# A two-block diffusion transformer step on one core: squares of the inner tiles moved to GpSimd, modulation sums spread in eighths

## The reference, cut to what matters

```python
cond = silu(c)
for i in range(2):
    mod = (cond @ ada_w[i] + ada_b[i])[:, None, :]
    sh1, sc1, g1, sh2, sc2, g2 = split(mod, 6)
    h = rmsnorm(x, norm_mix_g[i]) * (1.0 + sc1) + sh1
    y = rglru_mixer(h, ...) if i == 0 else dsa_mixer(h, ...)
    x = x + g1 * y
    h = rmsnorm(x, norm_ffn_g[i]) * (1.0 + sc2) + sh2
    x = x + g2 * (square(relu(h @ ffn_w1[i])) @ ffn_w2[i])
...
# second network, per layer
mod   = silu(c_2) @ w_mod_2[i] + b_mod_2[i]
mod_c = silu(c_ctx_2) @ w_mod_2[i] + b_mod_2[i]
# in rglru_mixer: the decay
log_a = -8.0 * r * softplus(-lam)
```

## Time and profile before

| | |
|---|---|
| median of 3 runs | 4178.69 us (4171.87 to 4182.22) |
| profiled execution, its time | 4176.06 us |
| its span | 4174.3 us |
| mean granted TensorE clock | 0.927 |
| PE busy | 3728.4 us (89%) |
| DVE busy | 1787.4 us (43%) |
| ACT busy | 1277.4 us (31%) |
| POOL busy | 1016.4 us (24%) |
| DMA, mean | 80 GB/s |

### The profile page before, as it was taken

How to read it: one execution, slowest core, us unless ns; L and a number is a source line. 1 busy time by engine, 2 the same in 40 slices (tenths; PEclk the granted TensorE clock), 3 DMA queues, 4 the chain that set the end, 5 groups by cost and what they waited for, 6 DMA issues and landing times. The chain is left out here.

```text
span 4174.3 us, 42210 instructions
## 1 busy us (share of the span) xinstructions
PE 3728.4 (89%) x17052; PEld 2731.1 (65%) x17052; DVE 1787.4 (43%) x3099; ACT 1277.4 (31%) x2258; POOL 1016.4 (24%) x920
## 2 busy tenths in 40 slices
PE   7998999878898898898869988799998999998997
PEld 3446878436477784455668885688887447756885
DVE  7637785275478854502334441412223104422223
ACT  1413222246222224524422222321113334533222
POOL 0223433120133330011034520322222111004443
PEclk8998999989999998989968879899999999999998
DMA  6425543110244431110011101111111111012221
GB/s 264 151 81 191 202 165 127 46 41 1 80 173 165 175 134 53 39 41 21 1 40 40 32 14 71 41 63 66 70 60 46 46 41 56 1 41 74 88 101 61
DMA packets 67043, 333.94 MB, mean 80 GB/s; under 512 B 32352, under 2 KB 35360, under 8 KB 42016
## 3 DMA queue, kind: packets, MB, share of 16 engines
q1 hardware_dynamic: 66416, 328.86, 21.4%
q10 hardware_dynamic: 432, 2.38, 0.1%
HBM read 324.30 MB, written 6.91 MB: 79 GB/s over the span
## 5 line engine op out<-in xcount | busy, mean ns | idle before, releaser
L629 PE MATMUL PSB<-R,R 128*128 128x512 f32 (+1 forms) x2432 | 929.4, 382 | 94.9 <-DVE R L887 48.9
L603 POOL TENSOR_TENSOR R<-SB,R 128x1024 fp32r<-128x1024 f32 x260 | 640.0, 2463 | 1420.5 <-ACT R L594 1420.4
L630 PE MATMUL PSB<-R,R 128*128 128x512 f32 (+1 forms) x2432 | 897.4, 377 | 0.0
L559 PE MATMUL PSB<-SB 128*128 128x512 f32 (+1 forms) x2176 | 843.3, 549 | 23.4 <-ACT SB L1285 18.5
L633 PE MATMUL PSB<-R,R 128*128 128x512 f32 (+1 forms) x2432 | 845.7, 377 | 0.0
L559 PEld LDWEIGHTS PSB<-SB 128*128 128x128 f32 x2176 | 420.7, 194 | 439.2 <-issue 409.7
L629 PEld LDWEIGHTS PSB<-R,R 128*128 128x128 f32 x2432 | 467.2, 192 | 219.3 <-DVE R L1011 31.9
L630 PEld LDWEIGHTS PSB<-R,R 128*128 128x128 f32 x2432 | 467.4, 192 | 79.6
L633 PEld LDWEIGHTS PSB<-R,R 128*128 128x128 f32 x2432 | 437.1, 193 | 65.3
L421 DVE SCALAR_TENSOR_TENSOR SB<-SB 128x512 f32<-128x512 f32 x504 | 473.6, 984 | 7.2 <-DMA SB<-in_ada 2.0
L594 ACT ACTIVATE R<-SB 128x1024 fp32r<-128x1024 f32 x260 | 273.2, 1052 | 551.3 <-PE PSB L633 532.7
(11 more groups left out here) (318 smaller groups left out, 4218.7 us busy)
## 6 DMA issues: line engine op xcount, KB each, us to landing
SB<-in_w SPq DMA_DIRECT2D x95, 2048.0 KB, 8.6
SB<-in_ada SPq DMA_DIRECT2D x96, 1024.0 KB, 5.1
SB<-gate_rows SPq DMA_DIRECT2D x12, 512.0 KB, 4.3
SB<-in_rpb SPq DMA_DIRECT2D x8, 448.0 KB, 3.3
spill<-SB SPq DMA_DIRECT2D x1, 3072.0 KB, 10.7
SB<-gate_rows SPq DMA_DIRECT2D x24, 128.0 KB, 3.8
SB<-spill SPq DMA_DIRECT2D x1, 3072.0 KB, 10.0
SB<-in_x SPq DMA_DIRECT2D x8, 256.0 KB, 4.9
```

The costliest lines, as they stand in the source:

```text
L559: ins = e.mm(banks[ring[(g + c) % len(ring)]][0:m, 0:n], t[:, 0:m], xs[k][:, lo:lo + n], k == 0, k == nkt - 1)
L603: e.tt(lr, t, hf, ALU.subtract).then_inc(*G.up(("lo", j), *done))
L629: e.mm(b[:, 0:n], wh, xh[:, lo:lo + n], x == 0, False)
L630: e.mm(b[:, 0:n], wh, xl[:, lo:lo + n], False, False)
```

## The change

Three parts. In both ffn1 stages the square of the rectified inner tile is taken by GpSimd, in its queue behind the split of the weight group two ahead. The modulation work is cut in eighths of a job (one slice of 512, for m=2 taken twice), called part here; part p of the stage is done at row `p * 60 // (8 * jobs)`, a row being one output tile of the stage, 64 in all; on VectorE it stands behind the tile's own steps, and TensorE sums a job at the head of the row two behind that of its last part. The load of a half goes to the row behind that in which the half two ahead is used up. In rglru the order of sums is written out and stays as it was; the half biases and the softplus stand ahead of the first modulation work on VectorE, and its Exp ahead of the squares on ScalarE.

```diff
+    def part(self, v, D, p):
+        j, i = divmod(p, 8)
+        t = p // 4
         cond, m = self.jobs[j][1:3]
         v.wait_ge(*self.landed(t))
...
+    def row_of(self, p):
+        return p * 60 // (8 * len(self.jobs))
+
+    def sp_row(self, e, r):
+        for t in range(2 * len(self.jobs)):
+            if (0 if t < 2 else self.row_of(4 * (t - 2) + 3) + 1) == r:
+                self.rows_in(e, t)
+
+    def pe_row(self, e, P, r):
+        for j in range(len(self.jobs)):
+            if self.row_of(8 * j + 7) + 2 == r:
+                self.pe_sum(e, P, j)
+
+    def dve_row(self, v, D, r):
+        for j in range(len(self.jobs)):
+            if self.row_of(8 * j + 7) + 2 == r:
+                self.dve_sum(v, D, j)
+        for p in range(8 * len(self.jobs)):
+            if self.row_of(p) == r:
+                self.part(v, D, p)
...
# ffn1, pe
-                                lambda x, lo: [st.at("h", x)], each=lambda x: x < 7 and fill.pe(e, at, P))
+                                lambda x, lo: [st.at("h", x)], each=lambda x: fill.pe_row(e, P, 16 * q + x))
...
# ffn1, dve
                     for mt in range(8):
-                        if mt < 7:
-                            fill.dve(v, at, D)
                         u = 8 * q + mt
-                        v.wait_ge(*st.at("relu", u))
-                        v.wait_ge(*(st.at("hid", (u - 3) // 8, (u - 3) % 8) if u >= 3 else st.at("h", 7)))
-                        v.tt(T[u % 3], R[u % 2], R[u % 2], ALU.mult).then_inc(*D.up(("hid_square", u)))
                         v.wait_ge(*st.at("hid_hi", u))
                         v.tt(HID[mt][2], T[u % 3], HID[mt][0], ALU.subtract).then_inc(*D.up(("hid", q, mt)))
+                        fill.dve_row(v, D, 16 * q + mt)
                         g += 1
                     for mt in range(8):
-                        if mt % 2:
-                            fill.dve(v, at, D)
                         v.wait_ge(*st.at("mm", g))
...
+                        fill.dve_row(v, D, 16 * q + 8 + mt)
...
# ffn1, pool
-                for j in range(hv.groups):
+                for j in range(2):
                     hv.pool(e, G, j)
+                for q in quarters:
+                    for mt in range(16):
+                        hv.pool(e, G, 16 * q + mt + 2)
+                        if mt < 8:
+                            u = 8 * q + mt
+                            e.wait_ge(*st.at("relu", u))
+                            e.wait_ge(*(st.at("hid", (u - 3) // 8, (u - 3) % 8) if u >= 3 else st.at("h", 7)))
+                            e.tt(T[u % 3], R[u % 2], R[u % 2], ALU.mult).then_inc(*G.up(("hid_square", u)))
...
# rglru, act
+                e.wait_ge(*st.at("minus_abs"))
+                e.act(z, z, ACT.Exp).then_inc(*A.up(("exp_minus_abs",)))
                 e.wait_ge(x_landed, 128)
...
# rglru, dve
+                v.ts(hb[:, 0:10], Pm["rb"], 0.5, None, ALU.mult).then_inc(*D.up())
+                v.ts(hb[:, 10:20], Pm["ib"], 0.5, None, ALU.mult).then_inc(*D.up(("half_bias",)))
+                softplus(v, D, s, Pm["lam"], -1.0, z, z2, m_, st.at)
...
                 for f in range(8):
                     v.stt(H[f], X[f], gs[:, f:f + 1], RX[:, 0:S], ALU.mult, ALU.mult).then_inc(*D.up(("scaled", f)))
-                v.ts(hb[:, 0:10], Pm["rb"], 0.5, None, ALU.mult).then_inc(*D.up())
-                v.ts(hb[:, 10:20], Pm["ib"], 0.5, None, ALU.mult).then_inc(*D.up(("half_bias",)))
-                softplus(v, D, s, Pm["lam"], -1.0, z, z2, m_, st.at)
```

More of the change, by code:

```diff
@@ L355, in landed @@
         return (self.early[t][1], 16) if t < len(self.early) else (self.sems[t % 2], 16 * (self.base + t // 2 + 1))
[L357 to L406, removed]
+    def rows_in(self, e, t):
+        if t >= len(self.early) + 2:
+            e.wait_ge(*self.st.at("half", t - 2))
+        q = self.jobs[t // 2][0]
+        e.load(self.slot(t), self.d_ada[q, :, (t % 2) * 2048:(t % 2 + 1) * 2048]).then_inc(self.landed(t)[0], 16)
+    def part(self, v, D, p):
+        j, i = divmod(p, 8)
+        t = p // 4
@@ L407, in dve @@
         cond, m = self.jobs[j][1:3]
         v.wait_ge(*self.landed(t))
-        if half == 0 and j >= 2:
+        if i == 0 and j >= 2:
             v.wait_ge(*self.st.at("modsum", j - 2))
[L411 to L426, removed]
+        w = self.slot(t)[:, (p % 4) * 512:(p % 4 + 1) * 512]
+        for x in range(m):
+            c = cond[:, i * m + x:i * m + x + 1]
+            acc = self.accs[x][j % 2]
+            ev = [("half", t), ("acc", j), ("acc_part", j, x)]
+            if i == 0:
+                v.ts(acc, w, c, None, ALU.mult).then_inc(*D.up(*ev))
+            else:
+                v.wait_ge(*self.st.at("acc_part", j, x))
+                v.stt(acc, w, c, acc, ALU.mult, ALU.add).then_inc(*D.up(*ev))
@@ new lines, in pe_sum, with dve_sum @@
+    def pe_sum(self, e, P, j):
+        m = self.jobs[j][2]
+        e.wait_ge(*self.st.at("acc", j))
+        if j:
+            e.wait_ge(*self.st.at("mod", j - 1))
+        for x in range(4):
+            for v in range(m):
+                e.mm(self.bank[:, x * m + v:x * m + v + 1], self.accs[v][j % 2][:, col(x)],
+                     self.ones[:, 0:1]).then_inc(*P.up(("modsum", j)))
+    def dve_sum(self, v, D, j):
+        _, _, m, bias, MOD = self.jobs[j]
+        v3 = lambda a: a.rearrange("p (j m) -> p j m", m=m)
+        v.wait_ge(*self.st.at("modsum", j))
+        v.tt(v3(MOD), v3(self.bank[:, 0:4 * m]), bias.unsqueeze(2).broadcast_to([128, 4, m]),
+             ALU.add).then_inc(*D.up(("mod", j)))
@@ L675, in sp @@
                     e.load(X[f], d_x[f, :, :]).then_inc(x_landed, 16)
-                at = fill.start()
-                for _ in range(8):
-                    fill.sp(e, at)
+                for t in range(8):
+                    fill.rows_in(e, t)
                 panels(e, "a_in", 0, 0)
@@ L816, in dve @@
                 for f in rows:
-                    fill.dve(v, at, D)
+                    if 10 + f in later:
+                        fill.dve_sum(v, D, later[10 + f])
+                    if f < 6:
+                        for i in range(4):
+                            fill.part(v, D, 72 + 4 * f + i)
                     v.wait_ge(*st.at("gate", 2 * f + 1))
                     v.stt(HS[f], M[f], 1.0, XCV[f], ALU.add, ALU.mult).then_inc(*D.up(("gated_x", f)))
-                fill.dve_flush(v, at, D)
                 for f in rows:
@@ L915, in sp @@
                 after(e, st)
-                at = fill.start()
-                for _ in range(2):
-                    fill.sp(e, at)
                 for q in quarters:
```

57 lines of the change are left out of this document (25 added, 32 removed).

## The result

The changed kernel takes 4246.3 us (median of 4 runs, 4239.0 to 4249.8) against 4180.5 for the kernel before in the same comparison (4171.9 to 4183.6): ratio 1.0159, interval 1.0138 to 1.0179, so 1.6% slower. The direction was forecast (4194, slower), the size was not: +66 us in place of +15, and outside the range (4158 to 4212).

The account below looks back on a forecast made before the run. VectorE was taken to bound the m=2 inner rows, TensorE the outer ones. Second ffn +12 and first ffn +3 made +15 us on 4178.7: 4194, 0.36% slower; range 4158 to 4212, likeliest case 4191 to 4210.

Parts of the forecast that it names:

- (a): Squares to GpSimd in both ffn stages: saves VectorE 0.68 us each, shuts it out 1.05; -1.4 to +0.4 us per row.
- its other price, 1.4: GpSimd's square at 1.4 us instead of 1.2, by the skill's 2x rule; 0.2 more a row, some 3 us altogether.
- (b): Parts over rows 0 to 59: at m=2 VectorE's inner rows fall from 9.4 to 6.9 us, still bounding against TensorE's 6.0.
- (c): Sum two rows on leaves VectorE 2.8 us for its parts; short by 1 to 5 us for two jobs in three.
- The walk: Row-by-row sum of both ffn stages with the steps' prices and pauses: second ffn +12 us, first +3.
- (d): Softplus first moves 5.8 us of small steps into VectorE's wait for the first in_ada: nothing, bounds -2 to +2 us.
- 1.9 us of half clock behind each pause of some 2 us or more: Charge in the row-by-row sum for TensorE's matmuls running at 1.2 instead of 2.4 GHz after each longer pause.
- a forecast of +3: First ffn ends about 743 against 739.8 us: window pauses at rows 4, 21, 24, 34; rows 32 to 47 gain 15.
- The relief wins: Rival: parts end before TensorE asks, only row budgets count; whole 4109, half 4144, quarter 4161 us; chance 0.25, mostly 4144 to 4166.
- GpSimd or the loads as a bound: Third rival: GpSimd's chain at 6.3 us a row or colliding loads cost 20 to 25 us more, 4217; chance 0.07.
- The signs named: In the ffn stages: sums' waits over 70 us, first some 11, square 1.2 to 1.3, row 47 early, row 63 late.
- two signs of being wrong: In the ffn stages: sums' waits under 40 us, or TensorE's rows past 50 costing what they cost before.

Follow-up runs that it names:

- four rows: The changed kernel with each job's sum four rows behind its last part instead of two; 4092.7 us, ratio 0.9795 to the kernel before.
- parts first: The changed kernel with an inner row's parts ahead of VectorE's subtraction; 4162.7 us with sums two rows on, 4112.5 us with sums four rows on.
- three rows: The changed kernel with each job's sum three rows behind its last part instead of two; 4124.6 us, ratio 0.9874 to the kernel before.

## Why the prediction was right in direction and wrong in size

- **(a) Squares.** The price was right: 1.29 us on GpSimd, and VectorE shut out for it. That they gain where there is room (16 us by themselves, 17 with four rows) and cost where there is little (35 with two rows, some 9 with three) was not seen; the bounds of -1.4 to +0.4 us a row held both signs, and which one holds is decided by the window. The Trainium skill ("SBUF — State Buffer", § Who interferes with whom) calls the SBUF port pair that VectorE and GpSimd share an exclusive lock. 9.07 us for six accumulates beside three GpSimd operations, 4.0 without, agree with it; but the conclusion drawn from it, that the relief "has no room", does not hold: it pays 17 us in a wide window, since `hid` comes sooner. The measured 1.29 lies between the prediction's 1.22 and its other price, 1.4; the "some 3 us over both stages" given for the latter does not come out of 0.2 us in each of 64 rows, which is 13. Nothing else in the sum hung on it.
- **(b) Parts spread.** VectorE's rows were priced with one row's GpSimd work, 3.1 us shut out. When VectorE is a row behind, two rows' work falls on one, and three parts at m=2 took 5.0 us more than alone, not 3.1. So row 47 was late where it was to be 8 us early: 1512.2, less the 15.9 by which the stage began later, is 1496.3 against 1478.9. By itself, with VectorE's squares (and the early softplus), the spread with its two-row sum costs 34 us. The accumulates' 1224 ns, where 1 us was expected, are mostly another matter: with four rows, where hardly anything waits, they still take 1198, with VectorE's squares 1173 (two rows) and 1156 (four). So of the 240 ns above the 984 of before most comes with the spreading and 40 to 50 with the squares on GpSimd. The prediction's own row prices say as much: 3.1 us for some 4.7 accumulates plus 2.1 and 1.05 are 1.3 us each.
- **(c) The window.** Right in mechanism and largely in size. The walk had 11.6 us at row 4, 4.4 at row 8, then 1.5, 4.9 and 8.1; the trace has 13.43, 4.86, then 1.2, 4.1 and 7.55. Over the second ffn the walk comes to 11.6 + 4.4 + 3 x 14.5 = 59.5 us, the trace to 66.1. That one number of the code (two rows) is worth 122 us when it is three and 154 when it is four. What the step missed is that the window of before was not two rows for every job: ten of the 18 sums of a stage stand two rows behind their last half, the other eight three to five, since `fill` is called in every second outer row only and not in the last inner one. All nine waits of before for its sums, in both stages, are at two-row ones (rows 5, 37, 52 of the first; 3, 5, 20, 22, 37, 52 of the second), and so are all seven where only the squares were moved. The change made every window two rows.
- **(d) Softplus.** Nothing, as forecast. Beside the earlier trace rows: the first accumulate now starts at 12.01 instead of 12.25.

```profile
12.01 0.49 DVE L375 TENSOR_SCALAR SB<-SB 128x512 f32<-128x512 f32 x1 [0.80 <-DMA SB<-in_ada]
```

- **The step that failed** is the term "1.9 us of half clock behind each pause of some 2 us or more". It was taken from one pause of 1.82 us in the first ffn, behind which the m=1 sum still ran near full pace (1.05 us for its eight, 0.95 without a pause). Behind the longer pauses of the changed kernel the sum itself runs at half clock (3.57 in place of 1.84), and pauses under 2 us can pay too (behind one of 1.58 us the sum took 3.21, behind another 2.74). In the second ffn the 18 sums take 51.8 us in place of 18 x 1.84 = 33.1, and 152 starts of the other matmuls lie some 0.43 apart in place of 0.227, 30 us more: 49 in all, against 10 by the same count with four rows. TensorE's busy time says about the same, 438.5 us against 395.5 with four rows: 43 us where the walk charged 8 pauses x 1.9 = 15. These 28, and the 6.6 of longer pauses (66.1 for 59.5), are the 34 by which the second ffn exceeded the forecast (+46 for +12). The trace of before showed it already, at the first sum of its second ffn, and this row was not used:

```profile
1144.06 3.57 PE L377 MATMUL PSB<-SB 128*128 128x1 f32 x16 [7.48 <-DVE SB L421]
```

- **The first ffn**, +13.7 us for a forecast of +3, failed in the same term. Its pauses were right in total: 15.7 us in the four that the walk named and 14.5 in its last quarter are 30.2, the trace has 30.1 (11.2, 3.2 in two that were not named, and 15.6). The half clock was charged six times, 11.4 us; TensorE's busy time, here for the changed kernel and then with four rows, differs by 22.3. That leaves 10.9, about the 10.7 by which the forecast was exceeded:

```profile
318.00:750.00 432.00, 398.96 (x1728) 327.45 (x1728) 313.29 (x293) 109.68 (x139) 200.45 (x95) 0.93 0.43 163
```

```profile
322.00:704.00 382.00, 376.68 (x1728) 311.57 (x1728) 313.47 (x290) 109.86 (x139) 199.86 (x95) 0.99 0.49 184
```

- **Not in the sum at all:** 15.6 us where no instruction changed. The stretch between the ffns took 373.1 to 375.8 us in ten of the profiles, that of before among them, and 378.5 to 379.9 in the four others; the one behind the second 2595.7 to 2613.3. TensorE's busy time differs by 5 of the changed kernel's 5.9, at a granted clock of 0.91 against 0.93. What sets this was not found, and one profile of each kernel cannot tell whether the kernel does or the single execution.
- **The rivals.** "The relief wins" was the same machine with the window open. Its whole was 4109; four rows reach 4092.7, with GpSimd's squares and all parts spread. It was stated as depending on where a part's end falls, which was right, and given 0.25; the code's two rows decided against it. GpSimd or the loads as a bound did not show: TensorE's waits in the second ffn name neither.
- **The signs named:** sums' waits over 70 us (96.2) and the first of about 11 (13.4), the square of 1.2 to 1.3, row 63 late, and L1011's successor gone from the top of TensorE's waits, came. Accumulates near 1 us and row 47 early did not. Of the two signs of being wrong neither came: the sums' waits were not under 40 us, and the rows past 47 took 123.7 us (1512.22 to 1635.95) where they had taken 95.0.

## What to carry to other kernels

When work is spread finer over an engine's loop, look at the distance between its last piece and whoever reads the result: count, in rows, what a piece can still meet on the way (here up to three parts and two rows of a shut-out port), and move the consumer back until a buffer's depth stops it. Here four rows in place of two turned +1.6% into -2.0% with the same work. Before judging an offload or an order within a row, open the window: in a tight one the sign of both was the opposite of what it was in a wide one (squares on GpSimd +35 and -17 us, parts first -84 and +20). And when a cost is taken from one row of a trace, look for the rows where it would be largest before it is multiplied.

## What the runs showed of the hardware beyond what was expected

- Sixteen one-column matmuls take 3.57 us at granted clock 0.50 and 1.84 at full.
- Pauses of TensorE cost half clock on top of the standing, but at no fixed rate. In the second ffn, standing and busy time of the same instructions: four rows 16.5 and 395.5 us, three rows 27.9 and 409.1, parts first (two rows) 38.2 and 423.2, only the squares moved 44.8 and 408.6, the changed kernel 68.5 and 438.5. Against four rows each us more of standing goes with 0.5 to 1.3 us more of busy time. What sets the rate is not shown.
- Spare matmuls in the pauses pay even when not all fit: 216 more matmuls, mean clock 0.93 instead of 0.86, stage 10.3 us shorter. The whole kernel was 23 us faster, but the rest of that lies where nothing was changed.
- The same instructions outside the changed stages differ by up to 7 us in 374 and by 18 in 2600 between profiles of kernels that differ elsewhere; the clock granted between the two ffns was 0.91 in the changed kernel and 0.93 before.
